# Six sums over partitions in a two-block transformer kernel: one-column products of TensorE in place of transposes and row sums on VectorE

## The reference

```
c_act = jax.nn.silu(c)
mod = jnp.dot(c_act, ada_w[l]) + ada_b[l]
sh1, sc1, g1, sh2, sc2, g2 = jnp.split(mod, N_MOD, axis=-1)
h = modulate(rms_norm_2(x, norm1_g[l]), sh1, sc1)        # h * (1 + sc1) + sh1
...
x = x + g1[:, None, :] * jnp.einsum('bsd,de->bse', merged, w_out[l])
```

## Time and profile before

| | us |
|---|---|
| median of three runs | 909.12 |
| lowest, highest | 904.49, 909.81 |
| the profiled execution | 908.68 |
| its span (first to last instruction) | 907.4 |
| TensorE busy (share of the span) | 893.5 (98%) |
| VectorE busy | 732.1 (81%) |
| ScalarE busy | 568.7 (63%) |

### The profile page before, as it was taken

One profiled execution on the slowest core, in us unless ns is written; L12 is line 12 of the kernel. 1 busy time (PEld: TensorE's weight loads), 2 busy tenths in 40 slices (PEclk: granted clock), 3 DMA queues, 4 the chain that ended last, 5 costly groups with the idle time before them and its releaser, 6 DMA issues.

```text
span 907.4 us, 18483 instructions
## 1 busy us (share of the span) xinstructions
PE 893.5 (98%) x7360; PEld 868.8 (96%) x7360; DVE 732.1 (81%) x1164; ACT 568.7 (63%) x830; POOL 1.9 (0%) x9
## 2 busy tenths in 40 slices
PE   8999999999999999999999999999999999999996
PEld 7999989999999999999999999899999999999996
DVE  6778998899998999898966999988689975555454
ACT  7848456775577787664446878677776754444541
POOL 0000000000000000000000000000000000000000
PEclk9999999999999999999999999999999999999998
DMA  8766555555875789998855566644455565655641
GB/s 317 254 190 227 153 159 177 163 186 202 282 255 168 261 296 347 342 331 307 328 186 176 170 216 204 196 155 138 143 164 185 163 210 186 186 186 187 189 137 47
DMA packets 53157, 189.83 MB, mean 209 GB/s; under 512 B 6208, under 2 KB 6864, under 8 KB 52944
## 3 DMA queue, kind: packets, MB, share of 16 engines
q1 hardware_dynamic: 52928, 188.65, 62.8%
q10 hardware_dynamic: 144, 0.00, 0.0%
HBM read 186.53 MB, written 1.05 MB: 207 GB/s over the span
## 4 chain that ended last, share of the span: by engine, by line
PE 89%; ACT 5%; DVE 4%; issue 1%; DMA 1%; SPq 0%; ACTq 0%; DVEq 0%
PE bank L1004 26%; PE bank L1006 26%; PE bank L1007 26%; PE bank L977 2%; PE bank L979 2%; PE bank L978 2%; ACT whi L1875 1%; DVE wlo L1042 1%; ACT gates L2320 1%; PE bank L710 1%; DMA raw<-in_stream 1%; PE bank L949 0%; PE bank L956 0%; PE bank L651 0%; PE bank L952 0%
## 5 line engine op out<-in xcount | busy, mean ns | idle before, releaser
L1042 DVE TENSOR_TENSOR wlo<-raw,whi 128x1024 fp32r<-128x1024 f32 x297 | 361.0, 1222 | 99.0 <-ACT whi L1875 98.0
L1875 ACT ACTIVATE whi<-raw 128x1024 fp32r<-128x1024 f32 x297 | 311.5, 1056 | 201.3 <-PE bank L1007 188.6
L1004 PE MATMUL bank<-Alo,whi 128*128 128x256 f32 x1344 | 378.4, 282 | 0.0
L1007 PE MATMUL bank<-Ahi,whi 128*128 128x256 f32 x1344 | 374.0, 278 | 0.0
L1006 PE MATMUL bank<-Ahi,wlo 128*128 128x256 f32 x1344 | 374.0, 278 | 0.0
L1004 PEld LDWEIGHTS bank<-Alo,whi 128*128 128x128 f32 x1344 | 252.7, 188 | 3.2 <-issue 2.7
L1007 PEld LDWEIGHTS bank<-Ahi,whi 128*128 128x128 f32 x1344 | 254.4, 189 | 0.0
L1006 PEld LDWEIGHTS bank<-Ahi,wlo 128*128 128x128 f32 x1344 | 252.4, 188 | 0.6 <-issue 0.2
L1007 PE MATMUL bank<-Fhi,whi 128*128 128x256 f32 (+1 forms) x320 | 88.8, 278 | 0.0
L1006 PE MATMUL bank<-Fhi,wlo 128*128 128x256 f32 (+1 forms) x320 | 88.8, 278 | 0.0
L1004 PE MATMUL bank<-Flo,whi 128*128 128x256 f32 x256 | 71.3, 278 | 0.0
(11 more groups left out here) (409 smaller groups left out, 1377.9 us busy)
## 6 DMA issues: line engine op xcount, KB each, us to landing
raw<-in_stream SPq DMA_DIRECT2D x298, 512.0 KB, 4.3
araw<-in_ada SPq DMA_DIRECT2D x48, 512.0 KB, 6.2
TB<-in_TB SPq DMA_DIRECT2D x1, 1536.0 KB, 7.2
a8r<-a SPq DMA_DIRECT2D x16, 64.0 KB, 3.8
bc<-in_bc SPq DMA_DIRECT2D x1, 896.0 KB, 6.3
out<-H SPq DMA_DIRECT2D x3, 256.0 KB, 2.2
H<-in_xT SPq DMA_DIRECT2D x1, 512.0 KB, 7.3
mats<-in_mats SPq DMA_DIRECT2D x1, 449.0 KB, 7.1
```

Source lines behind the costliest of these rows:

```text
L1004: pe.matmul(os[j], wh, xl, start=k == 0 and (wide or j == 0), stop=False, skip_group_check=not wide)
L1007: i = pe.matmul(os[j], wh, xh, start=False, stop=k == K - 1 if wide else last, skip_group_check=not wide)
L1042: v.tensor_tensor(wlo[:, s % NHL, :], raw[:, s % NRAW, :], whi[:, s % NHL, :].bitcast(F32), ALU.subtract).then_inc(*lo_v.up(s))
L1875: a.activation(whi[:, s % NHL, :], raw[:, s % NRAW, :], ACT.Copy).then_inc(*hi.up(s))
```

## The change

In task `sums` TensorE forms, for each 128 x 128 part of `aacc`, the product with one column of `ones`: the part is loaded as the weights, one column is streamed, and the result is one column of sums in bank 6. The eight columns of a block lie side by side. Bank 7 isn't used. VectorE then adds the bias to the eight columns on the way out of PSUM, with one instruction of 128 x 8 for each block. The bias addition over 48 columns goes, the `gains` part of the task follows in the same step as the last block, and those who waited for `mod_v("mod")` wait for `red_v` of block 5. The product into bank 5 behind each block stays.

```diff
-    "sums": (SUMS, [n + 1 for n in SUMS] + [SUMS[5] + 3], []),
+    "sums": (SUMS, [n + 1 for n in SUMS], []),
...
             def sums():
                 for cb in range(6):
-                    w.wait_ge(*mats_in.at("in"))
                     w.wait_ge(*ada_v.at(8 * cb + 7))
...
                     for j in range(8):
-                        i = pe.transpose(banks[6 + j // 4][:, j % 4 * 128:j % 4 * 128 + 128],
-                                         aacc[cb % 2][:, j * 128:j * 128 + 128], ident)
+                        i = pe.matmul(banks[6][:, j:j + 1], aacc[cb % 2][:, j * 128:j * 128 + 128], ones[:, 0:1],
+                                      start=True, stop=True)
                     i.then_inc(*ada_pe.up(cb))
                     pe.matmul(banks[5][:, 0:T], ones[:, :], mats[:, 0:T], start=True, stop=True)
...
             def sums():
                 for cb in range(6):
                     w.wait_ge(*ada_pe.at(cb))
-                    for j in range(2):
-                        i = v.tensor_reduce(mod[:, 8 * cb + 4 * j:8 * cb + 4 * j + 4],
-                                            banks[6 + j][:, :].rearrange("p (a c) -> p a c", a=4), AXX, ALU.add)
-                    i.then_inc(*red_v.up(cb))
-                    yield
+                    at = COFF["adab"] + 8 * cb
+                    v.tensor_tensor(mod[:, 8 * cb:8 * cb + 8], banks[6][:, 0:8], cols[:, at:at + 8], ALU.add
+                                    ).then_inc(*red_v.up(cb))
+                    if cb < 5:
+                        yield
                 w.wait_ge(*red_v.at(5))
-                v.tensor_tensor(mod[:, :], mod[:, :], cols[:, COFF["adab"]:COFF["adab"] + 48], ALU.add
-                                ).then_inc(*mod_v.up("mod"))
-                w.wait_ge(*mod_v.at("mod"))
+                w.wait_ge(*red_v.at(5))
...
-                    w.wait_ge(*mod_v.at("mod"))
+                    w.wait_ge(*red_v.at(5))
```

## The result

In the same measurement the changed kernel took a median of 914.85 us (911.25 to 918.81, ten runs) and the kernel before 909.38 us (903.30 to 910.48, ten runs). The ratio is 1.0094, with a 95% interval of 1.0065 to 1.0123. The forecast was 914.6 us. The profiled execution took 912.78 us with a span of 911.4, against 908.68 and 907.4 before.

What follows compares the result with a forecast made beforehand. The prediction took TensorE's queue to bound the kernel: 5.5 us more for one-column products, VectorE's relief counted as nothing, added to a 909.1 us median gave 914.6 us. The eight-in-ten range was 907 to 921 us.

Steps and rivals of the forecast that it cites:

- TensorE's queue is the path: Whole kernel: TensorE busy 98%, suppliers wait for it and not the reverse, so work added to it adds to the time.
- Two loads of 0.111 us per product: Six blocks: 16 loads take 1.78 us in place of 0.87 for the transposes, 5.5 us more in all.
- Rival 4: One-column products: a second instruction needs no load time, 0.89 us a block, TensorE as it was, 909.2 us; chance 0.03.
- rival 5: One-column products: four passes, each takes twice as long, 3.55 us a block, +16 us, 925 us; chance 0.01.
- rival 6: One-column products: column nearly free, loads hidden behind each other, 906.5 us halfway, 903.9 at most; chance 0.03.
- two passes: Plain 32-bit products: the trace was read as showing two passes where the skill's precision page has four.
- VectorE's terms: Row sums (7.7 us) and 48-column addition (0.20) go, six additions (1.0) come: 6.9 us relief, counted as nothing on the path.
- rival 3: VectorE's relief counts on the path: 6.9 us off the forecast, 907.7 us; chance 0.04.
- The pace: Main products start every 0.113 or 0.118 us; the forecast kept the short pace from block 1 to 492 us.
- Rival 1: Block 1 to 492 us: short pace lost, about 146 us of main products take 5.8 us more, 920.4 us; chance 0.16.
- The end: From 721.80 to about 898 us main products run at the long pace, 0.118 us; the forecast left this unchanged.
- Rival 2: From 721.80 to about 898 us: long pace flips to short, 7.0 us off, 907.6 us; chance 0.11.

## Why the prediction was right

- *TensorE's queue is the path.* Right. 5.5 us more work outside the main products lengthened the kernel, 6 us less on VectorE did nothing, as the run with transposes and the new VectorE part shows by itself.
- *Two loads of 0.111 us per product, 16 x 0.111 = 1.78 us a block, 5.5 us in all.* Right: 1.78 us at block 0, the rest 181.0 to 186.5 us; that the 5.5 comes out to the digit is luck, since the other profiles give 4.5 to 6.6. Half the products took it back (180.8), one instruction per product too (0.90 us for eight), and twice as many added 1.78 us at the full clock. Rivals 4, 5 and 6 fall with it. One reading of the prediction is wrong: two instructions don't mean two passes. The unread product, also two instructions, costs 0.43 us with 256 columns, about four times the 0.113 us of a main product, which fits four passes and not two; with one column the loads set the time, and the number of passes doesn't show. The Trainium skill's 60 cycles for 1 to 64 columns (page "TensorE: Matmul & The Clock Gate", section "Back-to-back issue gap") stand there for a single gap without a weight load, and don't apply where each product brings its own weights: the trace has 0.111 us.
- *VectorE's terms.* L1358 took 0.16 us, near the 0.17 assumed; 5.8 us of relief in place of 6.9, and none of it shortened the kernel (rival 3 falls). VectorE did not come to wait for TensorE.
- *The pace.* Rival 1, at 0.16, came true in part, and each time: three of the five stretches, behind blocks 1, 3 and 5. They hold 238, 262 and 310 main products; times 0.0044 us that is 3.6 us. 5.5 + 3.6 = 9.1 us, which is the difference of 908.68 and 917.8 (other stretches that differ, by up to 1 us, about cancel in it). Its reason was right in part: what stands ahead of the product into bank 5 does change the pace of what follows, but the same sequence gives the long pace at one block and the short one at the next. That I gave it 0.16 is the step that was wrong: I held the unchanged last product against it. I also read that a pace changes only where something small stands between the main products. In the kernel before it changed at 285.4 us with nothing between, 0.5 us behind one late step (0.18 us):

```profile
284.73 0.34 PE L1004 MATMUL bank<-Ylo,whi 128*128 128x256 f32 x1
284.91 0.28 PE L1006 MATMUL bank<-Yhi,wlo 128*128 128x256 f32 x1
```

- *The end.* Rival 2's mechanism is real, but it isn't an effect of the change: the end is short in some runs and long in others, in both kernels, and about 6 us hang on it.
- So the median of 914.6 was met partly by luck. In that measurement eight of ten runs of before lay in the upper group and five of ten of the change, which hid the 3.6 us that the forecast had left out. The change's own cost like for like is 8 to 10 us, about 1%, and the ratio of 1.0094 with its interval is nearer to this than the 5.5 us between the medians.

Not settled: what about a small sequence makes the pace short or long, and what differs between runs ahead of the end. Three simple rules (it turns over, it brings the short pace, the unread product alone decides) each met a case against it. Not tested: whether the place of the instructions in the program or the moment at which a sequence falls matters; every edit here that changed the sequence moved these too.

## What to carry to other kernels

On a TensorE that is never idle, count instructions and weight loads, not columns: a product of plain 32-bit numbers with one column costs two loads, and a transpose one. Before a change of a few microseconds is judged, count the main products per equal stretch in several profiles of both kernels; here the pace behind the change moved 3.6 us beside 5.5 us for the work in it, and the pace of a far-off stretch moved 6 us, by chance. Medians of runs in two groups say what the mixture is; compare group with group.

## What the runs showed of the hardware

- The same stream of weight load and 256-column product runs at 0.113 or 0.118 us per step at a granted clock of 1.00, holds its pace over up to 1486 steps, and changes it only at a short disturbance: a few 32-bit products or transposes, or a single late step (0.18 us at 284.73 in the kernel before).
- Cutting a tile of 8 bytes per partition out of a padding tile ahead of the activations put the whole stream at 0.118 us; that kernel was 1.9% slower than the one before (927.26 against 909.02 us), with less work on TensorE than the change. With the column inside the padding tile, the short pace came back.
- 32 one-column instructions in a row were followed by a granted clock at the 1.2 GHz level at all six blocks, though TensorE was busy throughout: 0.56 in the 5 us in which those of block 0 ended, after 1.00 in the 5 us ahead. At block 1 the clock was 1.00 during them (344 to 348 us) and 0.77 in the 2 us behind. 16 (1.78 us) did not do this.
- A plain 32-bit product is two instructions with a weight load each: 0.22 us with one column (16 loads in 1.78 us for eight products), 0.43 us with 256 columns (1.55 us with it, 1.11 us without). A 32-bit transpose of 128 columns is one, 0.109 us.
